# Half of the first feed-forward's gate product, by seven products of block sums instead of eight

## The chip, the cores and the metric

The kernel runs on one core of one Trainium2 chip. The metric is the device time in microseconds (us); three runs of the kernel before took 1800.26, 1800.73 and 1801.78 us, median 1800.73.

The engines are named as the profile names them: PE is TensorE (matrix multiplication), PEld its weight loading, DVE is VectorE, ACT is ScalarE, POOL is GpSimd, SP is SyncE, which here issues the DMAs (transfers from device memory). Each engine works through its own queue in order, and engines wait for each other on semaphores.

## The reference

Two blocks run one after the other on 512 tokens of 1024 features, in float32. Each feed-forward is two products with a gate between them; the change concerns the first one:

```python
def swiglu(x, w_gate, w_up, w_down):
    return (jax.nn.silu(x @ w_gate) * (x @ w_up)) @ w_down

def first_block(x, ...):
    ...                                   # input product, convolution and pooling groups
    h = h + y @ w_out[l]
    h = h + swiglu(rmsnorm(h, g_ffn[l]), w_gate[l], w_up[l], w_down[l])
    return rmsnorm(h, g_final)
```

`w_gate` and `w_up` are 1024 x 2816, `w_down` is 2816 x 1024. The second block has two layers of attention and feed-forward of the same sizes; they aren't touched.

## The kernel before

Features lie on the 128 partitions and tokens along the free dimension: `XH` and `XL` hold the normed input as eight tiles (the 1024 features) of 512 tokens. Precision comes from splitting each number in a high part, rounded to the matrix engine's format, and a low part, the remainder. A product is three matmuls: high weights by low input, high by high, low weights by high input (lines L983 to L985, helper `product`).

The stage "gu0" makes 22 tiles of gate and 22 of up, 128 hidden features each. One weight tile of 1024 x 128 is an *item*: 8 slices of the contraction by 3 matmuls, 24 matmuls of 512 tokens. Items come in the order gate, up, gate, up. The first two are made in halves of 256 tokens while the norm still delivers its halves (`stage_in_halves`, L1056 to L1069).

Each item passes through four engines:

- SP loads it to `raw`, which has 2 slots. Item g may be loaded when the low part of item g-2 is done (`w_lo`, helper `load`, L525 and L526).
- ACT rounds it to `WH` (helper `high`, two halves, L1605). It waits until it has landed and until PE is done with item g-4, as `WH` and `WL` have 4 slots.
- POOL subtracts to get `WL` (helper `low`, two halves, L742).
- PE multiplies.

Behind PE, ACT takes the silu of the gate bank (L1830), DVE multiplies it with the up bank to `hid` (L2428), ACT rounds that to `HH` (L1821) and POOL subtracts to `HL` (L869). `HH` and `HL` are the 22 hidden tiles that the product after this stage reads.

The norm ahead of the stage (`norm_in_halves`): DVE scales a tile of 256 tokens (L2156) into a small ring, ACT rounds to `XH` (L1658), POOL subtracts to `XL` (L783, `lows_of_halves`), and DVE may not go on with the ring until POOL has read it.

The order on each engine is written out by hand; in this stage it is a loop over pairs of tiles on every engine. Nothing reorders it.

Of the kernel before, what the change touches and what calls it, by code (L numbers as in the profile page):

```python
# [68 lines left out]

STAGES = {}  # L70
_item, _turn = 0, DT
for _name, _n, _t in (("in", 12, 12), ("out", 8, 8), ("gu0", 2 * FT, 2 * FT), ("down0", 8 * len(DOWN), 8),
                      ("qkv1", 4 * UNITS, 4 * UNITS), ("out1", 8, 8), ("gu1", 2 * FT, 2 * FT),
                      ("down1", 8 * len(DOWN), 8), ("qkv2", 4 * UNITS, 4 * UNITS), ("out2", 8, 8),
                      ("gu2", 2 * FT, 2 * FT), ("down2", 8 * len(DOWN), 8)):
    STAGES[_name] = (_item, _turn)
    _item, _turn = _item + _n, _turn + _t
# [88 lines left out]
class Chain:  # L166
# [9 lines left out]
    def sync(self, but=0):  # L176

        if self.it is None:
            self.eng.wait_ge(self.sem, self.count - but)
        else:  # L180
            self.eng.wait_ge(self.sem, self.it * self.per + self.count)
# [16 lines left out]
def two_blocks(nc, A, out):  # L198
    ctx = ExitStack()
    with ctx:  # L200
# [36 lines left out]
        pairs_of = [work[:, i, :].rearrange("p (a s) -> p a s", a=2) for i in (0, 1, 4)]  # L237
# [34 lines left out]
        ffn.close()  # L272
        att = ExitStack()
# [45 lines left out]
        sc = [pb("score0"), pb("score1")]  # L319
        tb = [pb("turned0"), pb("turned1")]  # L320
# [91 lines left out]
        slots = [*h_lo, *hid_ready, *ex, *pt_l, *o_read, qk_lo, sub_lo, sum_tiles]  # L412
# [60 lines left out]
        def ff_banks(it, j):  # L473

            return ob if isinstance(it, int) and j == 1 else bank

# [44 lines left out]
        def _(sp):  # L521
# [71 lines left out]
            stage("gu0", FT // 2, 4, pairs(w_gate, w_up))  # L593
# [135 lines left out]
        def _(pool):  # L729
# [143 lines left out]

            lows("out")
            lows_of_halves(1, "gu0")
            lows_of_hidden("gu0", 0)
# [104 lines left out]
        def _(pe):  # L981
# [97 lines left out]

            def gate_and_up(name, m):  # L1080

                stage_in_halves(name, m)
# [508 lines left out]
        def _(act):  # L1591
# [25 lines left out]
            def norm_in_halves(m, follower=None, gain=None):  # L1617
# [31 lines left out]
                def tops(h, p, tiles=range(2)):  # L1649
# [3 lines left out]
                    for t, w in TILES_OF_HALF:  # L1653
# [3 lines left out]
                        src = pairs_of[(DT * h + t) // 2 % 3][:, t % 2:t % 2 + w, :] if m == 1 else xres[:, t:t + w, c]  # L1657
# [160 lines left out]
            def hidden_hi(it, j, name):  # L1818

                act.wait_ge(bank_read[1], Nth(STAGES[name][1] + 2 * j + 1, it, 4).round(2, 1))  # L1820
                act.activation(HH[:, bass.ds(it * 2 + j, 1), :], hid[:, j:j + 1, :], ACT.Copy).then_inc(h_hi, 1)  # L1821
# [3 lines left out]
            def gate_hidden(it, j):  # L1825
                g = Nth(STAGES["gu0"][0] + 2 * j, it, 4)
                act.wait_ge(item_done, g.n(1))

                act.wait_ge(bank_read[1], Nth(STAGES["gu0"][1] + 2 * j + 1, it, 4).round(2, -1))
                act.activation(act_g[:, j, :], ff_banks(it, j)[0][:, :], ACT.Silu).then_inc(bank_read[0], 1)  # L1830
                high(g + 3)
                hidden_hi(it, j, "gu0")
                high(g + 4)

            for j in range(2):
                gate_hidden(0, j)
            with act.Fori(1, FT // 2) as it:
                for j in range(2):
                    gate_hidden(it, j)
# [232 lines left out]
        def _(dve):  # L2072
# [53 lines left out]
            def norm_in_halves(name, factor, gain, in_place=False):  # L2126
# [17 lines left out]
                def pair(h, p):  # L2144
                    c = slice(h * HALF, (h + 1) * HALF)
                    i = DT // 2 * h + p
                    dst = pairs_of[i % 3]
                    if p == 0:
                        dve.wait_ge(rstd_wide, stat(n, h))
                    if not centred:  # L2150
                        if i >= 3 and not in_place:
                            dve.wait_ge(x_lo, DT + half_tile(m, 0, 2 * (i - 3)) + 2)
                        for j in range(2):
                            t = 2 * p + j
                            x = xres[:, t, c]
                            dve.scalar_tensor_tensor(out=x if in_place else dst[:, j, :], in0=x, scalar=pcol(gain, t),  # L2156
# [266 lines left out]
            def gate_hidden(it, j):  # L2423
                g, u = Nth(STAGES["gu0"][0] + 2 * j + 1, it, 4), Nth(STAGES["gu0"][1] + 2 * j, it, 4)
# [257 lines left out]
```

## Time and profile before

| | |
|---|---|
| median of 3 runs | 1800.73 us |
| the profiled execution | 1802.1 us |
| its span | 1800.3 us |
| mean granted clock of TensorE | 0.995 |
| PE busy | 1761.6 us, 98% of the span |
| POOL, ACT, DVE busy | 1030.7, 796.4, 754.2 us (57%, 44%, 42%) |
| DMA | 171.93 MB, mean 96 GB/s |
| stage gu0 in this execution | 155.7 to 398.5 us |

Times in the profile are counted from the start of the span; 1.8 us of the execution lie outside it. A matmul's shown duration is longer than its distance from the next one, since matmuls are pipelined. So what a matmul costs is read from the distance between starts. The same holds in a smaller way for ACT and DVE: in a row "x2" the total is less than twice the duration of one.

### The profile page before, as it was taken

How to read it: one execution, taken by the hardware profiler on the slowest of the kernel's cores; microseconds unless marked ns; L12 is line 12 of the kernel's file. 1: busy time of each engine (PE TensorE's matmuls, PEld its weight loads, DVE VectorE, ACT ScalarE, POOL GpSimd, SP SyncE). 2: the span in 40 equal slices, each digit the busy share in tenths (PEclk: the TensorE clock that was granted, in tenths of full speed). 3: DMA queues.
4: the chain of work that ended last, by engine and by line, in shares of the span. 5: the costliest groups of instructions: out<-in, count | busy, mean ns of one | idle time of the engine just before them, and what ended most of it. 6: DMA issues, size and time to landing. Idle time of an engine off the chain costs nothing.

```text
span 1800.3 us, 26803 instructions
## 1 busy us (share of the span) xinstructions
PE 1761.6 (98%) x8755; PEld 1475.7 (82%) x8755; DVE 754.2 (42%) x1318; ACT 796.4 (44%) x1674; POOL 1030.7 (57%) x926
## 2 busy tenths in 40 slices
PE   8999999999999999999999999999999999999997
PEld 6879888888887888788888888878887888888887
DVE  7963000002235556453333322477875533333224
ACT  5644233232245555464444422466665644444231
POOL 6966555555562333466666665566564666666651
PEclk9999999999999999999999999999999999999999
DMA  4312333323234554323333333333332233332332
GB/s 153 94 44 80 104 101 93 93 79 114 87 88 114 136 123 122 88 72 109 100 93 95 88 105 92 87 82 88 88 84 79 71 106 93 96 102 79 105 92 98
DMA packets 327251, 171.93 MB, mean 96 GB/s; under 512 B 43458, under 2 KB 316948, under 8 KB 327188
## 3 DMA queue, kind: packets, MB, share of 16 engines
q1 hardware_dynamic: 327172, 171.12, 33.9%
q8 instruction: 35, 0.57, 0.1%
q14 instruction: 28, 0.23, 0.0%
q10 hardware_dynamic: 16, 0.00, 0.0%
HBM read 152.15 MB, written 2.10 MB: 86 GB/s over the span
## 4 chain that ended last, share of the span: by engine, by line
PE 86%; DVE 5%; POOL 3%; ACT 3%; issue 1%; DMA 1%; SPq 1%; DVEq 0%; ACTq 0%; POOLq 0%
PE bank L983 24%; PE bank L985 23%; PE bank L984 23%; PE attended L983 2%; PE attended L984 2%; PE attended L985 2%; PE turned L1424 1%; POOL WL L742 1%; PE attended L1440 1%; PE bank L1056 1%; PE bank L1068 1%; POOL psums L805 1%; ACT pmap L1861 1%; DVE small L2454 1%; DVE xres L2165 1%
## 5 line engine op out<-in xcount | busy, mean ns | idle before, releaser
L742 POOL TENSOR_TENSOR WL<-raw,WH 128x512 fp32r<-128x512 f32 (+3 forms) x656 | 775.7, 1204 | 540.9 <-ACT WH L1605 538.2
L983 PE MATMUL bank<-XL,WH 128*128 128x512 f32 x1432 | 568.4, 397 | 3.8 <-DVE work L2577 1.3
L985 PE MATMUL bank<-XH,WL 128*128 128x512 f32 x1432 | 557.6, 389 | 0.0
L984 PE MATMUL bank<-XH,WH 128*128 128x512 f32 x1432 | 556.9, 389 | 0.0
L1605 ACT ACTIVATE WH<-raw 128x512 fp32r<-128x512 f32 (+3 forms) x656 | 338.5, 566 | 296.3 <-PE bank L985 189.6
L985 PEld LDWEIGHTS bank<-XH,WL 128*128 128x128 f32 x1432 | 269.2, 188 | 56.9
L983 PEld LDWEIGHTS bank<-XL,WH 128*128 128x128 f32 x1432 | 269.7, 188 | 55.7 <-DVE work L2577 1.6
L984 PEld LDWEIGHTS bank<-XH,WH 128*128 128x128 f32 x1432 | 269.9, 188 | 50.2
L983 PE MATMUL bank<-HL,WH 128*128 128x512 f32 (+1 forms) x528 | 198.6, 376 | 0.0
L985 PE MATMUL bank<-HH,WL 128*128 128x512 f32 (+1 forms) x528 | 198.4, 376 | 0.0
L984 PE MATMUL bank<-HH,WH 128*128 128x512 f32 (+1 forms) x528 | 198.4, 376 | 0.0
L869 POOL TENSOR_TENSOR HL<-hid,HH 128x512 f32 x66 | 85.1, 1290 | 70.7 <-ACT HH L1821 70.7
L2366 DVE SCALAR_TENSOR_TENSOR xres<-xres,bank 128x512 f32 (+1 forms) x27 | 18.6, 687 | 249.7 <-PE bank L985 247.0
L983 PEld LDWEIGHTS bank<-HL,WH 128*128 128x128 f32 x528 | 99.4, 188 | 18.1
L984 PEld LDWEIGHTS bank<-HH,WH 128*128 128x128 f32 x528 | 99.4, 188 | 18.0
L985 PEld LDWEIGHTS bank<-HH,WL 128*128 128x128 f32 x528 | 99.3, 188 | 18.0
L1861 ACT ACTIVATE pmap<-score,small 128x128 f32<-128x128 f32 (+3 forms) x128 | 67.2, 525 | 93.6 <-DVE small L2454 92.2
L2428 DVE TENSOR_TENSOR hid<-bank,act_g 128x512 f32<-128x512 f32 x21 | 14.5, 692 | 207.5 <-PE bank L985 203.9
L1959 ACT ACTIVATE hid<-bank,par 128x512 f32<-128x512 f32 x42 | 32.7, 778 | 143.6 <-PE bank L985 143.6
L2514 DVE SCALAR_TENSOR_TENSOR hid<-bank,par,hid 128x511 f32<-128x511 f32 x42 | 31.5, 749 | 150.8 <-ACT hid L1959 150.6
L2514 DVE SCALAR_TENSOR_TENSOR act_g<-bank,par,act_g 128x511 f32<-128x511 f32 x42 | 31.5, 750 | 133.9 <-ACT act_g L1959 133.9
L2454 DVE TENSOR_REDUCE small<-score 128x1 f32<-128x128 f32 (+3 forms) x128 | 62.2, 487 | 40.1 <-PE score L1409 27.7
(365 smaller groups left out, 2508.7 us busy)
## 6 DMA issues: line engine op xcount, KB each, us to landing
raw<-in_ffn_w_in SPq DMA_DIRECT2D x88, 512.0 KB, 3.7
raw<-in_w_gate SPq DMA_DIRECT2D x22, 512.0 KB, 3.7
raw<-in_w_up SPq DMA_DIRECT2D x22, 512.0 KB, 3.7
raw<-in_ffn_w_out SPq DMA_DIRECT2D x28, 384.0 KB, 3.2
raw<-in_ffn_w_out SPq DMA_DIRECT2D x28, 320.0 KB, 3.1
raw<-in_a_w_in SPq DMA_DIRECT2D x16, 512.0 KB, 3.9
raw<-in_kv_w SPq DMA_DIRECT2D x32, 256.0 KB, 3.0
raw<-in_w_in SPq DMA_DIRECT2D x12, 512.0 KB, 3.7
```

Of the source, the lines that this page charges most:

```text
L742: pool.tensor_tensor(wl, x, wh, ALU.subtract).then_inc(w_lo, 1)
L805: own.link(pool.tensor_tensor(dst[:, PAD:], src[:, PAD:], src[:, PAD - d:PAD + S - d], ALU.add))
L869: pool.tensor_tensor(HL[:, bass.ds(it * 2 + j, 1), :], hid[:, j:j + 1, :], HH[:, bass.ds(it * 2 + j, 1), :].bitcast(F32), ALU.subtract).th ...
L983: pe.matmul(out_, wh, xl, start=start, stop=False)
L984: pe.matmul(out_, wh, xh, start=False, stop=False)
L985: return pe.matmul(out_, wl, xh, start=False, stop=stop)
L1605: act.activation(wh, x, ACT.Copy).then_inc(w_hi, 1)
L1861: act.activation(pmap[:, n % 4, 0:k], sc[c][:, 0:k], ACT.Exp, bias=small[:, n % 4:n % 4 + 1], accum_out=small[:, 4 + n % 4:5 + n % 4]).the ...
L1959: act.activation(dst[:, j, :], ff_banks(it, j)[side][:, :], ACT.Identity, bias=ff_par(layer - 1, 3, n), scale=ff_par(layer - 1, 2, n)).the ...
L2366: dve.scalar_tensor_tensor(out=r, in0=r, scalar=factor, in1=src[j][:, :].rearrange("p (a s) -> p a s", a=1), op0=ALU.mult, op1=ALU.add).th ...
L2454: dve.tensor_reduce(small[:, n % 4:n % 4 + 1], sc[c][:, 0:(n // 2 + 1) * P], AX_X, ALU.max, negate=True).then_inc(mx[c], 1)
L2514: own.link(dve.scalar_tensor_tensor(out=dst[:, j, 1:], in0=src[:, 0:S - 1], scalar=ff_par(layer - 1, 1, n), in1=dst[:, j, 1:], op0=ALU.mul ...
```

## The change

The input tiles 0 to 7 and the tokens form blocks: for a pair of input tiles (2k, 2k+1) and the two halves of the tokens, four blocks B11, B12, B21, B22; for two neighbouring gate tiles and the same two input tiles, four blocks of weights. The product of two such 2 x 2 arrangements is normally eight block products. In the variant of Winograd it is seven, of sums of blocks. A *quad* below is this for one k: seven products, each 3 matmuls of 256 tokens; four quads (k = 0 to 3) make the gate for two tiles. Seven of the eleven pairs of gate tiles (hidden tiles 2 to 15) are made so. Pair 0 and pairs 8 to 10, and all up tiles, are made as before.

What is added:

- Once: four sums of input blocks of 128x1024 on DVE (`turn_x`), their high parts on ACT (`turned_x_high`), their low parts on DVE (`turned_x_low`), between the norm and the first quad. They are kept in `TH` and `TL`, which are the hidden tiles 14 to 21 of `HH` and `HL`. The normed input is now written to `x_full` (hidden tiles 6 to 13), not to the ring.
- For each quad: a load of 256 KB (two input tiles by 256 weight columns) in place of one of 512 KB for each gate tile, so four small loads for two large ones; three sums and three plain blocks of weights. DVE makes four sums of weights in PSUM in three instructions (`quad_sums`) and their low parts (`sums_low`, 128x512); ACT makes the high parts of three plain blocks (`quad_high`, 128x384) and of the sums (`sums_high`, 128x512); POOL makes the low parts of the three plain blocks (`quad_low`, 128x384).
- For each pair: ACT copies the product P1 from PSUM (128x256), DVE combines the seven results in five instructions (`quad_answer`), then ACT takes the two silu.

```diff
-            stage("gu0", FT // 2, 4, pairs(w_gate, w_up))
+            folded("gu0", w_gate, w_up)
...
+                        if k < 4:
+                            src = wa[:, 2 * k:2 * k + 2, bass.ds(n, 2 * P)]
+                            sp.wait_ge(w_lo, g.times(2).n(2 * (1 - RAW)))
...
-                        src = pairs_of[(DT * h + t) // 2 % 3][:, t % 2:t % 2 + n, :] if m == 1 else xres[:, t:t + n, c]
+                        src = full_x(m)[:, t:t + n, c]
...
+                def quad(it, a):
+                    for k in range(4):
...
+                        for to, b, x, first in ((p1, 0, b11, True), (p2, 2, b21, True), (p4, 1, t4, True), (p7, 3, t3, True),
+                                                (p6, 5, t2, False), (p3, 6, b22, False), (p5, 4, t1, False)):
+                            if b == 0:
+                                if k == 0:
+                                    pe.wait_ge(quad_read, quad_count(name, it, a, 2).n() + OPEN)
+                                pe.wait_ge(w_lo, g.times(2).n(2))
+                            if b == 1 and k == 0:
+                                pe.wait_ge(t_lo, 4 * FOLDED.index(name) + 4)
+                            if b == 3:
+                                pe.wait_ge(sum_lo, q.n(1))
+                            mm = product(to, WHQ[:, s, b, :], WLQ[:, s, b, :], *x, first and k == 0, k == 3 and b >= 3)
...
+                item(Nth(STAGES[name][0] + 3), 0, XH, XL, 0, DT, True, True)
+                pe.wait_ge(bank_read[0], STAGES[name][1] // 2 + 2)
+                quad_pairs(pe.Fori, quad_pair)
...
+            def gate_quads(it, a, last):
...
+                high(quad_item("gu0", it, a, 4))
+                high(quad_item("gu0", it, a, 5))
...
+                    quad_high(next_item(0))
+                    sums_high(next_item(0), next_quad(0))
+                    quad_high(next_item(1))
+                act.wait_ge(item_done, quad_item("gu0", it, a, 3).n(1))
+                act.activation(p1_copy, ob[0][:, 0:HALF], ACT.Copy).then_inc(p1_out, 1)
                 for j in range(2):
-                    gate_hidden(it, j)
+                    act.wait_ge(quad_out, quad_count("gu0", it, a, 2, j).n(1))
+                    act.activation(act_g[:, j, :], answer[j][:, :], ACT.Silu).then_inc(quad_read, 1)
...
+                    sums_high(next_item(1), next_quad(1))
+                    quad_high(next_item(2))
+                hidden_hi(quad_tile(it, a, 0), 0, quad_turn("gu0", it, a, 0))
+                if not last:
+                    sums_high(next_item(2), next_quad(2))
+                    quad_high(next_item(3))
+                    sums_high(next_item(3), next_quad(3))
+                hidden_hi(quad_tile(it, a, 1), 1, quad_turn("gu0", it, a, 1))
...
+            def quad_sums(g, q):
+
+                r, to = raw[:, g.slot(RAW), 0:4, :], sums_of(q)
...
+                own.link(dve.tensor_tensor(to[:, 0:2, :], r[:, 0:1, :].broadcast_to([P, 2, P]), r[:, 1:3, :], ALU.add))
+                own.link(dve.tensor_tensor(to[:, 2, :], to[:, 1, :], r[:, 1, :], ALU.add))
+                dve.tensor_tensor(to[:, 3, :], to[:, 2, :], r[:, 3, :], ALU.add).then_inc(sum_ready, 1)
...
+                next_quad(0, quad_sums)
+                quad_answer("gu0", it, a)
+                next_quad(0, sums_low)
+                next_quad(1, quad_sums)
+                next_quad(1, sums_low)
+                next_quad(2, quad_sums)
+                value(0)
+                next_quad(2, sums_low)
+                next_quad(3, quad_sums)
+                value(1)
+                next_quad(3, sums_low)
```

On POOL a turn of the loop is `low` of the two up items, `quad_low` of the next quads 0 to 2, `HL` of the first hidden tile, `quad_low` of the next quad 3, `HL` of the second (`quad_lows`, `hidden_low`).

On PE, from the end of the fourth item on. Before, the loop over items of 512 tokens begins there:

```order
L985 MATMUL attended1<-XH,WL 128x512
L1085 UNCONDITIONAL_BRANCH
L1085 ISA
L990 ISA [waits bank_read0]
L983 MATMUL bank0<-XL,WH 128x512 [waits w_lo]
L984 MATMUL bank0<-XH,WH 128x512
L985 MATMUL bank0<-XH,WL 128x512
```

Now the first quad stands there (the first two of its seven products and the start of the third):

```order
L1127 MATMUL bank0<-XH,WL 128x512
L548 UNCONDITIONAL_BRANCH [waits bank_read0]
L548 ISA
L1238 ISA [waits quad_read]
L1125 MATMUL attended0<-XL,WH 128x256 [waits w_lo]
L1126 MATMUL attended0<-XH,WH 128x256
L1127 MATMUL attended0<-XH,WL 128x256
L1125 MATMUL turned<-XL,WH 128x256
L1126 MATMUL turned<-XH,WH 128x256
L1127 MATMUL turned<-XH,WL 128x256
L1125 MATMUL turned<-HL,WH 128x256 [waits t_lo]
```

The matmuls have 256 columns where they had 512, and there is a wait for the silu of the gate tile before (`bank_read0`), for the results' readers (`quad_read`), for the sums of the input (`t_lo`) and, three products on, for the sums of the weights (`sum_lo`). `HH` and `HL` stand for `TH` and `TL` here.

On ACT, from the norm's end to the first gate tile's silu and on. Before:

```order
L1658 ACTIVATE XH<-work 128x2x256 [waits xn_ready] x2
L1609 ACT_TABLE_LOAD
L1609 ACTIVATE small<-small 128x1
L1830 ACTIVATE act_g<-bank0 128x512 [waits bank_read1,item_done]
L1605 ACTIVATE WH<-raw 128x512 [waits item_done,w_landed1]
L1605 ACTIVATE WH<-raw 128x512
L1821 ACTIVATE HH<-hid 128x512 [waits bank_read1]
L1605 ACTIVATE WH<-raw 128x512 [waits item_done,w_landed0]
L1605 ACTIVATE WH<-raw 128x512
L1830 ACTIVATE act_g<-attended0 128x512 [waits bank_read1,item_done]
```

Now (from the same place; the norm, the table, item 3's high part and the high part of the first input sum stand ahead of these rows):

```order
L2035 ACTIVATE act_g<-bank0 128x512 [waits item_done]
L2023 ACTIVATE HH<-score 128x1024 [waits t_full]
L2013 ACTIVATE WH<-raw 128x384 [waits item_done,w_landed0]
L2023 ACTIVATE HH<-turned 128x1024 [waits t_full]
L2023 ACTIVATE HH<-score 128x1024 [waits t_full]
L2028 ACTIVATE HH<-hid 128x512 [waits bank_read1]
L2018 ACTIVATE WH<-score 128x512 [waits sum_ready]
L2013 ACTIVATE WH<-raw 128x384 [waits item_done,w_landed1]
L2018 ACTIVATE WH<-score 128x512 [waits sum_ready]
L2035 ACTIVATE act_g<-attended0 128x512 [waits item_done]
```

Between the silu of the first gate tile and that of the second there now stand the high parts of three of the input sums and of the first two quads, and the second silu (of `attended0`) is what `bank_read0` above waits for.

## Rows read from the trace of the kernel before

**Rows 1.** The page: busy time of each engine (share of the span), instructions

```profile
PE 1761.6 (98%) x8755; PEld 1475.7 (82%) x8755; DVE 754.2 (42%) x1318; ACT 796.4 (44%) x1674; POOL 1030.7 (57%) x926
```

**Rows 2.** Waits, 190 to 390 us: who for whom, us in total, times, longest

```profile
DVE hid L2428 <- PE bank L985: 193.8, 19, 10.4
```

**Rows 3.** PE in order of time: start, us, line, idle before in brackets

```profile
167.96 0.50 PE L1056 MATMUL bank<-XL,WH 128*128 128x256 f32 x2 [0.21 <-POOL XL L783]
169.98 0.40 PE L983 MATMUL attended<-XL,WH 128*128 128x512 f32 x1
...
180.89 0.39 PE L983 MATMUL bank<-XL,WH 128*128 128x512 f32 x1
...
398.49 0.39 PE L983 MATMUL bank<-HL,WH 128*128 128x512 f32 x1
```

**Rows 4.** PE in order of time, a stretch of matmuls of 256 columns

```profile
517.74 0.28 PE L984 MATMUL attended<-HH,WH 128*128 128x256 f32 x1
...
520.13 0.28 PE L1068 MATMUL bank<-XH,WH 128*128 128x256 f32 x1
```

**Rows 5.** DVE in order of time, 161 to 182 us

```profile
161.93 2.44 DVE L2156 SCALAR_TENSOR_TENSOR work<-xres,par,turned 128x256 f32<-128x256 f32 x6 [1.45 <-PE turned L1168]
...
166.22 0.48 DVE L2080 MEMSET work<- 128x512 f32 x1
...
170.86 0.69 DVE L2428 TENSOR_TENSOR hid<-bank,act_g 128x512 f32<-128x512 f32 x1 [3.61 <-ACT act_g L1830]
```

**Rows 6.** ACT in order of time, the first silu of the stage

```profile
170.06 0.60 ACT L1830 ACTIVATE act_g<-bank 128x512 f32<-128x512 f32 x1 [1.66 <-PE bank L1056]
```

**Rows 7.** POOL in order of time, 163 to 176 us

```profile
163.83 5.32 POOL L783 TENSOR_TENSOR XL<-work,XH 128x256 fp32r<-128x256 f32 x6
171.26 2.55 POOL L742 TENSOR_TENSOR WL<-raw,WH 128x512 fp32r<-128x512 f32 x2 [2.11 <-ACT WH L1605]
```

**Rows 8.** DVE in order of time, 504 to 507 us, where POOL works too

```profile
504.86 1.67 DVE L2373 TENSOR_TENSOR work<-work 128x512 f32<-128x512 f32 x1
```

**Rows 9.** POOL in order of time, 500 to 511 us

```profile
500.78 2.54 POOL L742 TENSOR_TENSOR WL<-raw,WH 128x512 fp32r<-128x512 f32 x2 [2.46 <-ACT WH L1605]
504.18 6.08 POOL L742 TENSOR_TENSOR WL<-raw,WH 128x512 fp32r<-128x512 f32 x4 [0.86 <-ACT WH L1605]
```

**Rows 10.** DVE groups by form: busy us, mean ns of one, idle before

```profile
L2458 DVE TENSOR_TENSOR PTL<-turned,PTH 128x512 fp32r<-128x512 f32 x24 | 16.4, 685 | 4.2 <-ACT PTH L1866 4.2
L2458 DVE TENSOR_TENSOR PTL<-turned,PTH 128x256 fp32r<-128x256 f32 x24 | 10.1, 421 | 5.7 <-ACT PTH L1866 5.7
L2458 DVE TENSOR_TENSOR PTL<-turned,PTH 128x128 fp32r<-128x128 f32 x24 | 6.9, 287 | 5.4 <-ACT PTH L1866 5.4
```

**Rows 11.** ACT groups by form, the same columns

```profile
L1727 ACT ACTIVATE work<-xin 128x1024 f32<-128x1024 f32 x4 | 4.2, 1058 | 2.7 <-DMA xin<-in_x 2.5
L1605 ACT ACTIVATE WH<-raw 128x384 fp32r<-128x384 f32 x111 | 54.3, 520 | 192.7 <-PE bank L985 152.9 <-DMA raw<-in_ffn_w_out 24.3 <-DMA raw<-in_w_down 15.6
L1866 ACT ACTIVATE PTH<-turned 128x256 fp32r<-128x256 f32 x24 | 9.0, 376 | 1.9 <-PE turned L1424 1.9
```

**Rows 12.** POOL in order of time, 385 to 440 us

```profile
400.50 1.29 POOL L869 TENSOR_TENSOR HL<-hid,HH 128x512 f32 x1 [3.44 <-ACT HH L1821]
...
433.29 1.99 POOL L742 TENSOR_TENSOR WL<-raw,WH 128x384 fp32r<-128x384 f32 x2 [1.92 <-ACT WH L1605]
```

**Rows 13.** ACT in order of time, the HH that Rows 12's first row waits for

```profile
399.68 0.63 ACT L1821 ACTIVATE HH<-hid 128x512 f32 x1 [4.71 <-DVE hid L2428]
```

**Rows 14.** DMA issues: KB each, us from issue to landing

```profile
raw<-in_w_gate SPq DMA_DIRECT2D x22, 512.0 KB, 3.7
...
raw<-in_kv_w SPq DMA_DIRECT2D x32, 256.0 KB, 3.0
...
QX<-work SPq DMA_DIRECT2D x32, 128.0 KB, 2.3
...
raw<-in_b_w_q SPq DMA_DIRECT2D x16, 256.0 KB, 3.3
```

More of the change, by code:

```diff
@@ L180, in sync @@
         else:
-            self.eng.wait_ge(self.sem, self.it * self.per + self.count)
+            self.eng.wait_ge(self.sem, self.it * self.per + (self.count - but))
     def link(self, ins):
@@ L475, in ff_banks, with t_banks, quad_item, quad_turn @@
             return ob if isinstance(it, int) and j == 1 else bank
+        folds, p1_copy = [work[:, 0, :], work[:, 1, :]], work[:, 4, 0:HALF]
+        answer = [tb[1], folds[0]]
+        def t_banks(n):
+            x = turned2 if n in (2, 0) else score2
+            return x[:, :, :].rearrange("p b s -> p (b s)").rearrange("p (k c) -> p k c", c=HALF)
+        turn_of_sums = [x.rearrange("p (b c) -> p b c", c=P) for x in sc]
+        def quad_item(name, it, a, k):
+            return Nth(STAGES[name][0] + 4 + QUAD_ITEMS * a + k, it, 2 * QUAD_ITEMS)
+        def quad_turn(name, it, a, j):
+            return Nth(STAGES[name][1] + 4 + 2 * a + j, it, 4)
+        def quad_count(name, it, a, per, k=0):
+            return Nth(per * (QUADS * FOLDED.index(name) + a) + k, it, 2 * per)
+        def plain_item(name, it, k):
+            return Nth(STAGES[name][0] + (QUAD_ITEMS - 4) * QUADS + k, it, 4)
+        def plain_turn(name, it, k):
+            return Nth(STAGES[name][1] - 2 * QUADS + k, it, 4)
+        def quad_tile(it, a, j):
+            return bass.ds(it * 4 + (2 * a + 2 + j), 1)
+        def sums_of(q):
+            return turn_of_sums[q.slot(2)]
+        def full_x(m):
+            return x_full if m == 1 else xres
+        def quad_pairs(Fori, part):
+            with Fori(0, QUAD_LOOP) as it:
+                for a in range(2):
+                    part(it, a, False)
+            part(QUAD_LOOP, 0, True)
         def first_unit(u):
@@ L1835, in _, with quad_high, sums_high @@
-            for j in range(2):
-                gate_hidden(0, j)
-            with act.Fori(1, FT // 2) as it:
-                for j in range(2):
-                    gate_hidden(it, j)
+            def quad_high(g):
+                s = g.slot(SLOTS)
+                act.wait_ge(w_landed[g.slot(RAW)], g.round(RAW, 1) * 16)
+                act.wait_ge(item_done, g.n(1 - SLOTS))
+                act.activation(WHQ[:, s, 0:3, :], raw[:, g.slot(RAW), 1:4, :], ACT.Copy).then_inc(w_hi, 1)
+            def sums_high(g, q):
+                act.wait_ge(sum_ready, q.n(1))
+                act.activation(WHQ[:, g.slot(SLOTS), 3:7, :], sums_of(q), ACT.Copy).then_inc(w_hi, 1)
```

277 lines of the change are left out of this document (242 added, 35 removed).

## The prediction

> **What bounds the kernel now.** I read the page first: PE is busy for 98% of the span, POOL for 57%, no other engine for half [rows 1]. Then the waits inside the stage: DVE waits for PE for 193.8 us in 200, and no row there has PE waiting for anyone [rows 2]. So at present every matmul taken out of this stage shortens the kernel by its full distance to the next, and the other engines have air. Then PE in order of time, to get prices and the stage's edges. The halves end at 169.98 (PE waited 0.21 us for POOL's `XL` shortly before), the fourth item ends at 180.89, the stage at 398.49 [rows 3]. Between 180.89 and 398.49 stand 40 items of 24 matmuls: 217.60 / 960 = 0.2267 us each, 5.44 us an item, 21.76 us a pair of tiles.
>
> **The price of a matmul of 256 columns.** From 517.74 to 520.13 there are 20 of them, 0.1195 us each [rows 4]. That is 5% more than half of 0.2267, so halving the columns costs something.
>
> **What is taken from PE.** For a pair the gate was 48 x 0.2267 = 10.88 us. Now it is 4 quads x 21 matmuls x 0.1195 = 10.04 us. The gain is 0.84 us for a pair, 5.9 us for seven. This is all that can be won: 0.33% of the kernel. What can be told from no change here is about 0.2%, 3.6 us. So 2.3 us of new waits on PE already hide the gain.
>
> **The start of the first quad.** Three things are new there.
>
> - DVE scales eight tiles for the second half of the tokens from 161.93 on, 2.44 / 6 = 0.41 us each, without the ring's wait now: until 165.2, with two fills of 0.48 us until 166.2 [rows 5]. Then comes the first sum of inputs, 128x1024 with both inputs in SBUF, while POOL makes the `XL` that PE waits for (its row runs from 163.83 to 169.15) [rows 7]. A DVE instruction of that kind took 1.67 us beside a busy POOL, where the same size with one input in PSUM takes 0.69 [rows 8, 10]; POOL needed 6.08 us for the four subtractions around it and 2.54 for two undisturbed ones, so it lost 1.0 [rows 9]. I read it as a lock: each waits for the other's instruction to end. The new sum is about 1.2 us long (0.685 at 512, and 0.26 more for each 256 [rows 10]), and POOL, and with it PE, come 1.2 us later: the halves end at 171.2, item 3 at 182.1.
> - The Trainium skill, SBUF — State Buffer, section "SBUF: two separate sides", states this as a rule: the port pair is an exclusive lock for a whole instruction, also for a DVE instruction with two SBUF inputs against a GpSimd one that reads SBUF. By that rule, the trace agrees; without it the end of the sum below would be 2.7 us earlier.
> - The chain to the first quad. DVE's first `hid` began 0.88 us after the halves' end [rows 3, 5], now at 172.1, and takes 0.69. Behind it stand two more input sums and four low parts, six instructions of 1024 at 1.24: 180.2. ACT's four high parts (1.06 each [rows 11]) fit between. Then the sums of quads 0 and 1, each 0.42 + 0.29 + 0.29 and small gaps, 1.05: 182.3. ACT makes the high part of quad 1's sums (0.60, as a read of PSUM [rows 6]) and only then the silu of `attended0` (0.60), for which PE waits: with three handovers 183.8. PE stands still for 1.7 us. The quads start 2.9 us later than their place before.
>
> If nothing else waited, the stage would end at 183.8 + 7 x (10.04 + 10.88) + 12 x 5.44 = 395.5, which is 3.0 us sooner.
>
> **The ring behind PE.** A pair now asks PE for 20.92 us only. But the preparation of one pair hangs in a ring, because each engine works in order: two `raw` slots, ACT's silu between weight copies, DVE's sums between answers. I walk it once, from POOL's first half of the first up item's low part to the same one of the next pair:
>
> 1. POOL, four half subtractions of 1.27 [rows 9]: 5.1 us. They free the slot for quad 1's load.
> 2. The load of 256 KB. Not in this form in the trace: 512 KB take 3.7, 256 KB in short rows 3.0 to 3.3, 128 KB in long rows 2.3 [rows 14]. The new one has rows of 1 KB, twice as long as the loads of 3.0; I take 2.5, nearer the long rows, and 2.7 with the handovers.
> 3. ACT: quad 1's plain high part, 0.42 to the next start (0.52 long), and the P1 copy, 0.38, queued behind it [rows 11]; with the handover 0.95. The copy was possible at the end of quad 3, and waits here for a load it has no need of.
> 4. DVE's five instructions of the answer: 0.69, 0.42, 0.42, 0.69, 0.42, with the overlap of independent ones 2.5 [rows 10].
> 5. DVE: low part of quad 0's sums 0.62, sums of quad 1 1.05: 1.7.
> 6. ACT's high part of these sums 0.60, two handovers, DVE's low part 0.62: 1.4.
> 7. DVE: sums of quad 2 1.05, `hid` 0.69: 1.7.
> 8. ACT: `HH` 0.53, high part of quad 2's sums 0.60, handovers: 1.35.
> 9. DVE: low part 0.62, sums of quad 3 with a wait of 0.25 for POOL 1.3, `hid` 0.69: 2.6.
> 10. ACT's `HH` 0.63, POOL's `HL` 1.29, handovers of 0.14, an estimate, and 0.19 (400.31 to 400.50) [rows 12, 13]: 2.25. Then POOL is at step 1 again.
>
> The sum is 22.25. The second up item's high part comes 0.15 late for POOL (its load starts only after POOL's last part of quad 3): 22.4 us a turn. That is 1.5 more than PE asks for, and 0.6 more than the 21.76 of before. For the first turn there is slack; then PE waits each turn, at quad 3 (POOL's part), at the first up item and at the next first quad.
>
> **The sum.** In pair 0, quad 2's load goes out when POOL is done with quad 0 (182.6) and lands at 185.2; its sums and low part take until 187.4 (1.05, then 1.0, half of the 1.99 for two of 128x384 [rows 12]); the up item's load (3.7) lands at 191.2; POOL starts on it at 192.0. Six turns later, at 192.0 + 134.4 = 326.4, POOL starts on the last quad pair's up item, PE on it 1.3 us later, and from there nothing waits: 14 items x 5.44 = 76.2. The stage ends at 403.9, against 398.5: 5.4 us later. Behind it PE still has no slack, so all of it reaches the end. The profiled execution (span 1800.3 and 1.8 around it, 1802.1) would come to 1807.5; it lies 1.4 us above the median, so the median is forecast at 1806.1 us.
>
> **Bounds.** The load between 2.3 (128 KB in long rows) and 3.3: minus 0.2 to plus 0.8 a turn. The Trainium skill, DMA: Bandwidth & Descriptors, section "Anatomy of one DMA", fits about 2.0 us plus the bytes at 436 GB/s, which would be 2.6 here and 0.6 us more in the sum; its 3.2 for 512 KB is under the measured 3.7. The ten handovers I set at 0.06 to 0.15, under the two that rows show (0.20 from 170.66 to 170.86 [rows 5, 6], and the 0.19 above); 0.05 more or less for each is 0.5 a turn either way. No wait for POOL at step 9: minus 0.25. So a turn is 21.45 to 23.7, and six turns move the end from 5.7 us below the forecast to 7.8 above it. At the low bound the ring gives 398.2, no change.
>
> **Rivals.**
>
> - *PE stays the limit* (the ring at 20.9 or less): 395.5, minus 3.0, 1797.7 us; if the start cost nothing as well, minus 5.9, 1794.8. For it: ACT's, DVE's and POOL's work for a pair sums to about 10, 12 and 12 us, none near 21. Against it: it isn't the sums that bind but the order in which they wait for each other.
> - *The ring is about as long as a pair was* (21.5 to 22.0): 1800 to 1804, no change to be told. For it: both handovers that the rows show stand where an engine has several waits or an address to work out, and a plain one may be shorter than I set it. This is the nearest case.
> - *The matmuls of 256 columns cost more in the loop than at 517 us*, since each quad has its own waits: 588 of them at 0.130 would be 6.2 us more and eat the whole gain with PE itself as the limit, 1804. Against it: the cost of a satisfied wait can't be seen in 40 items at 5.44. That the seven products bring less than 1/8 is the same question; the difference in count is certain.
> - *A longer load decides* (3.0 or more, as 256 KB in short rows): a turn of 22.9, plus 8.4, 1809.
>
> **How the numbers follow.** The forecast case with the longer load (slower by over 0.2%): 0.55. Of that the longer load is 0.15. No change, mostly the second rival: 0.31. PE the limit and the start cheaper than worked out, by which alone more than 3.6 us are won: 0.14. The range reaches from 1798.5 to 1811.5: below it lies most of "PE stays the limit", above it only both upper bounds at once. The likeliest case's own range is 1804.3 to 1811.
>
> **What would show it.** In the profile after: 588 matmuls of 256 columns in the stage at about 0.12 apart (else the gain is wrong). PE idle about 1.2 us more for `XL` near 168, and about 1.7 us for the silu of `attended0` near 182. From the second quad pair on, PE idle in each turn behind POOL's low parts, and a pair every 22.4 us; if a pair takes 20.9, the ring is wrong and the kernel is not slower. The load of 256 KB at 2.5. DVE's 1024-wide sum at 167 longer than 1.2. All stages behind as long as before; if they aren't, I have missed something outside the stage.

## The result, and the profile after

| | median, us | runs | ratio to before |
|---|---|---|---|
| before | 1801.26 | 4 | |
| changed | 1812.38 | 4 (1809.86 to 1812.68) | 1.0058 (1.0040 to 1.0075) |
| changed, once more, later | 1811.08 | 4 (1806.45 to 1811.84) | 1.0048 (1.0031 to 1.0065) |

The ratios are taken over all runs of both kernels and can differ a little from the quotient of the two medians. The kernel became slower by about 0.5%. 1806.1 was forecast, with 1811.5 as the upper end: the sign was right, the size about half of what was measured.

The profiled execution of after took 1809.86 us, with a span of 1808.0. Its first 160 us (the front), where the work on TensorE is the same, ran 2.1 us faster than in the profile of before, so times are compared from a point of the stage on. Most of that is TensorE's clock: the granted clock was 0.50, the level of 1.2 GHz, from 103.7 to 110.5 us in before's execution and from 104.8 to 108.2 in after's, with TensorE busy throughout, and half of the 3.4 us between the two is 1.7 us of its work. In the stage itself neither profile has such a stretch. The page of after, which answers to [rows 1]:

```profile
PE 1757.2 (97%) x9007; PEld 1479.2 (82%) x9007; DVE 831.0 (46%) x1473; ACT 818.5 (45%) x1713; POOL 1026.0 (57%) x927
```

PE is busy for 4 us less, in a span that is 8 us longer. The waits of after, 160 to 420 us (who for whom, us in total, times, longest), answer to [rows 2]:

```profile
PE attended L1125 <- POOL WL L978: 4.4, 6, 0.8
PE attended L1125 <- ACT act_g L2058: 2.8, 5, 1.1
PE bank L1125 <- DVE hid L2737: 1.7, 1, 1.7
PE bank L1125 <- POOL WL L841: 1.5, 6, 0.4
```

Before, PE waited in this stretch for `XL` only, 0.4 us in all. Now PE waits in every turn of the ring for POOL (L978, L841), in five of them for the silu (L2058), and once at its end (`hid`). The 1.3 us for `XL` and the 1.2 for the second silu of the start (L2035) come on top. PE in order of time, as in [rows 3] (start, duration, and the idle time before in brackets):

```profile
166.79 0.51 PE L1198 MATMUL bank<-XL,WH 128*128 128x256 f32 x2 [1.17 <-POOL XL L882]
168.81 0.40 PE L1125 MATMUL attended<-XL,WH 128*128 128x512 f32 x1
...
181.04 0.38 PE L1125 MATMUL attended<-XL,WH 128*128 128x256 f32 x1 [1.16 <-ACT act_g L2035]
...
247.96 0.38 PE L1125 MATMUL attended<-XL,WH 128*128 128x256 f32 x1 [0.39 <-ACT act_g L2058]
256.16 0.39 PE L1125 MATMUL attended<-XL,WH 128*128 128x256 f32 x1 [0.78 <-POOL WL L978]
259.08 0.50 PE L1125 MATMUL bank<-XL,WH 128*128 128x512 f32 x1 [0.18 <-POOL WL L841]
...
340.22 0.49 PE L1125 MATMUL bank<-XL,WH 128*128 128x512 f32 x1 [1.69 <-DVE hid L2737]
...
405.63 0.39 PE L1125 MATMUL bank<-HL,WH 128*128 128x512 f32 x1
```

I call the time from the product that waits for `XL` (here 166.79) to the first product with `HL` (405.63) the stage's length. It was 398.49 - 167.96 = 230.53 us before and is 238.84 now, 8.3 more; with 1.0 more of wait ahead of it the change costs 9.3 us. Behind the stage 1402.4 us remain, against 1401.8 before.

The ring, read from POOL's first part of the first up item of each pair (first, second and last of the seven):

```profile
189.50 5.05 POOL L841 TENSOR_TENSOR WL<-raw,WH 128x512 fp32r<-128x512 f32 x4 [0.54 <-ACT WH L1795]
211.61 2.53 POOL L841 TENSOR_TENSOR WL<-raw,WH 128x512 fp32r<-128x512 f32 x2
...
325.94 2.54 POOL L841 TENSOR_TENSOR WL<-raw,WH 128x512 fp32r<-128x512 f32 x2
```

Six turns take 136.44 us, 22.74 each. The loads, 180 to 330 us (KB each, us from issue to landing), answer to [rows 14]:

```profile
raw<-in_w_up SPq DMA_DIRECT2D x14, 512.0 KB, 3.6
raw<-in_w_gate SPq DMA_DIRECT2D x26, 256.0 KB, 2.7
```

One turn on ACT (from the plain high part of the next quad 0 to the silu of this pair) and on DVE:

```profile
240.42 0.53 ACT L2013 ACTIVATE WH<-raw 128x384 fp32r<-128x384 f32 x1 [2.00 <-DMA raw<-in_w_gate]
241.58 0.60 ACT L2018 ACTIVATE WH<-score 128x512 fp32r<-128x512 f32 x1 [0.63 <-DVE score L2704]
243.55 0.53 ACT L2013 ACTIVATE WH<-raw 128x384 fp32r<-128x384 f32 x1 [1.38 <-DMA raw<-in_w_gate]
243.99 0.36 ACT L2055 ACTIVATE work<-attended 128x256 f32<-128x256 f32 x1
246.72 0.60 ACT L2058 ACTIVATE act_g<-turned 128x512 f32<-128x512 f32 x1 [2.36 <-DVE turned L2728]
```

```profile
244.48 0.69 DVE L2724 TENSOR_TENSOR work<-work,turned 128x512 f32<-128x512 f32 x1 [2.94 <-ACT work L2055]
```

The third and fourth rows of ACT are the heart of it. The P1 copy (L2055) comes right behind a weight part that waited 1.38 us for its load, and DVE stood still for 2.94 us until the copy was there.

### The profile page after: what moved, and what is told of

Read it like the earlier page. It is cut to its first block, busy times and chain, and to the rows that moved or that the text cites. A ratio compares the mean times of both kernels' runs of the same rounds, so it can differ in the third digit from the quotient of the medians.

```text
span 1808.0 us, 27685 instructions
## 1 busy us (share of the span) xinstructions
PE 1757.2 (97%) x9007; PEld 1479.2 (82%) x9007; DVE 831.0 (46%) x1473; ACT 818.5 (45%) x1713; POOL 1026.0 (57%) x927
## 4 chain that ended last, share of the span: by engine, by line
PE 78%; DVE 8%; POOL 5%; ACT 3%; issue 3%; DMA 2%; DVEq 0%; SPq 0%; POOLq 0%; ACTq 0%
PE bank L1125 21%; PE bank L1127 21%; PE bank L1126 21%; POOL WL L841 3%; PE attended L1125 2%; PE attended L1127 2%; PE attended L1126 2%; PE turned L1614 2%; PE attended L1630 1%; DMA raw<-in_w_gate 1%; PE bank L1198 1%; PE bank L1210 1%; POOL psums L904 1%; DVE score L2702 1%; DVE xres L2418 1%
## 5 line engine op out<-in xcount | busy, mean ns | idle before, releaser
L841 POOL TENSOR_TENSOR WL<-raw,WH 128x512 fp32r<-128x512 f32 (+2 forms) x628 | 741.5, 1203 | 529.3 <-ACT WH L1795 527.0
L1125 PE MATMUL bank<-XL,WH 128*128 128x512 f32 (+1 forms) x1328 | 528.6, 398 | 7.3 <-POOL WL L841 2.0
L1127 PE MATMUL bank<-XH,WL 128*128 128x512 f32 (+1 forms) x1328 | 517.1, 389 | 0.0
L1126 PE MATMUL bank<-XH,WH 128*128 128x512 f32 (+1 forms) x1328 | 516.5, 389 | 0.0
L1795 ACT ACTIVATE WH<-raw 128x512 fp32r<-128x512 f32 (+2 forms) x628 | 322.5, 563 | 317.4 <-PE bank L1127 178.8
L1125 PEld LDWEIGHTS bank<-XL,WH 128*128 128x128 f32 x1328 | 250.1, 188 | 56.9 <-POOL WL L841 3.1
L1127 PEld LDWEIGHTS bank<-XH,WL 128*128 128x128 f32 x1328 | 249.7, 188 | 53.1
L1126 PEld LDWEIGHTS bank<-XH,WH 128*128 128x128 f32 x1328 | 250.3, 188 | 45.7
L978 POOL TENSOR_TENSOR WL<-raw,WH 128x384 fp32r<-128x384 f32 x28 | 28.5, 1016 | 71.2 <-DVE score L2704 71.2
L882 POOL TENSOR_TENSOR XL<-xres,XH 128x256 fp32r<-128x256 f32 (+1 forms) x48 | 43.7, 923 | 38.0 <-ACT XH L1848 38.0
```

The costliest lines, as they stand in the source:

```text
L841: pool.tensor_tensor(wl, x, wh, ALU.subtract).then_inc(w_lo, 1)
L882: pool.tensor_tensor(XL[:, t:t + n, c], src, XH[:, t:t + n, c].bitcast(F32), ALU.subtract).then_inc(x_lo, n)
L978: pool.tensor_tensor(WLQ[:, s, 0:3, :], raw[:, g.slot(RAW), 1:4, :], WHQ[:, s, 0:3, :].bitcast(F32), ALU.subtract).then_inc(w_lo, 2)
L1125: pe.matmul(out_, wh, xl, start=start, stop=False)
L1126: pe.matmul(out_, wh, xh, start=False, stop=False)
L1127: return pe.matmul(out_, wl, xh, start=False, stop=stop)
```

## The experiments

"Stage" is the length defined above. "PE waits" is the sum of the rows of PE in the waits, 150 to 420 us, the one for `XL` included. "Turn" is the mean of the six turns in the profile. The kernels ran in groups beside runs of before, whose medians are 1801.93 (23 runs, for e1 to e4), 1802.84 (21, e5 to e8) and 1802.07 (7, e9 and e10).

| kernel | median | ratio (interval) | stage | PE waits | turn |
|---|---|---|---|---|---|
| changed | 1812.38 | 1.0058 (1.0040 to 1.0075) | 238.84 | 12.9 | 22.74 |
| e1_copy_ahead | 1799.75 | 0.9985 (0.9975 to 0.9994) | 229.97 | 5.6 | 21.19 |
| e2_last_ahead | 1808.38 | 1.0028 (1.0015 to 1.0041) | 237.28 | 11.2 | 22.80 |
| e3_three_pairs | 1807.01 | 1.0028 (1.0018 to 1.0037) | 235.19 | 6.2 | |
| e4_silu_ahead | 1813.05 | 1.0062 (1.0045 to 1.0079) | 242.85 | 14.8 | 23.07 |
| e5_both_orders | 1797.09 | 0.9974 (0.9963 to 0.9984) | 226.32 | 2.6 | 20.99 |
| e6_all_waits | 1797.90 | 0.9977 (0.9965 to 0.9988) | 228.66 | 3.1 | 20.93 |
| e7_sum_behind_xl | 1812.55 | 1.0050 (1.0034 to 1.0067) | 240.94 | 12.7 | 22.71 |
| e8_half_load | 1806.41 | 1.0014 (1.0004 to 1.0023) | 234.56 | 9.5 | 22.13 |
| e9_start_in_order | 1794.54 | 0.9958 (0.9941 to 0.9975) | 224.98 | 1.5 | 20.96 |
| e10_changed_again | 1811.08 | 1.0048 (1.0031 to 1.0065) | 238.27 | 11.8 | 22.61 |

### The copy ahead of the load (e1)

```diff
+                def copy_p1():
+                    act.wait_ge(item_done, quad_item("gu0", it, a, 3).n(1))
+                    act.activation(p1_copy, ob[0][:, 0:HALF], ACT.Copy).then_inc(p1_out, 1)
...
                     quad_high(next_item(0))
                     sums_high(next_item(0), next_quad(0))
+                    copy_p1()
                     quad_high(next_item(1))
-                act.wait_ge(item_done, quad_item("gu0", it, a, 3).n(1))
-                act.activation(p1_copy, ob[0][:, 0:HALF], ACT.Copy).then_inc(p1_out, 1)
```

(In the last pass `copy_p1` stays where it was.)

> ACT's copy of P1 stands ahead of the plain high part of the next pair's quad 1, so it no longer waits for that quad's load; the last pair is as it was. Theory (the ring through POOL, DMA, ACT and DVE sets the stage's pace, and this copy is a link of it): a turn of the ring, read as the distance of POOL's first subtraction of a pair's first up item to the next pair's, falls by about 1.5 us from 22.7 to 21.2; PE's waits at a next first quad and at quad 3 shrink, and the stage is about 7 us shorter than in the changed kernel, which leaves it 2 to 4 us slower than before. Rival 1 (the matmuls of 256 columns or the start cost it): nothing moves in the loop, under 0.5 us. Rival 2 (the slot of the raw weights alone sets the pace): the turn stays at 22.7, because the loads go out when they did.

The turn is 21.19 us, as the theory had it, and of the ring's waits of PE 1.3 us of 8.7 are left in the whole stage. The stage is 8.9 us shorter, where 7 were expected, so the kernel isn't 2 to 4 us slower than before but a little faster. The same place on ACT:

```profile
301.35 0.53 ACT L2013 ACTIVATE WH<-raw 128x384 fp32r<-128x384 f32 x1 [1.94 <-DMA raw<-in_w_gate]
302.50 0.60 ACT L2018 ACTIVATE WH<-score 128x512 fp32r<-128x512 f32 x1 [0.62 <-DVE score L2708]
302.99 0.38 ACT L2049 ACTIVATE work<-attended 128x256 f32<-128x256 f32 x1
304.30 0.53 ACT L2013 ACTIVATE WH<-raw 128x384 fp32r<-128x384 f32 x1 [0.92 <-DMA raw<-in_w_gate]
305.83 0.60 ACT L2062 ACTIVATE act_g<-turned 128x512 f32<-128x512 f32 x1 [1.00 <-DVE turned L2732]
```

The copy no longer has a load in front of it, the answer is made while that load is under way, and the silu comes 4.5 us behind the first row where it came 6.3 behind. No instruction is saved and none made shorter. One instruction in another place moved the kernel from 0.5% slower to 0.15% faster, so the order, and not the work, set the length of a turn.

### The last pair (e2)

```diff
                 if last:
-                    high(next_item(0))
-                    high(next_item(1))
-                else:
+                if not last:
...
                 if last:
+                    high(next_item(0))
+                    high(next_item(1))
                     high(next_item(2))
```

> In the last pair of quads only, ACT's two rounds of the next plain items' weights are put behind the copy of P1 and the two silu. Theory (the 1.7 us that PE waited for DVE's hid at 340 us came from the copy queued behind two weight loads that had not landed): that wait goes, the stage is 1.7 to 2.1 us shorter than in the changed kernel and nothing else moves, ring turns stay at 22.7. Rival (PE waited there for weights as well, which now come later): the wait is replaced by one for POOL's subtraction of the first plain item, gain under 0.5 us.

The wait for `hid` at the end of the ring is gone from PE's waits, and the turns are as long as in the changed kernel. The stage is 1.6 us shorter (1.0 against e10's). The two medians differ by more, 2.7 to 4.0 us, which the profiles don't account for; the execution profiled here was the slowest of e2's eight (1811.46). What happened there, in the last pass of the changed kernel (ACT, then DVE):

```profile
332.36 1.16 ACT L1795 ACTIVATE WH<-raw 128x512 fp32r<-128x512 f32 x2 [3.28 <-DMA raw<-in_w_gate]
335.01 1.15 ACT L1795 ACTIVATE WH<-raw 128x512 fp32r<-128x512 f32 x2 [1.50 <-DMA raw<-in_w_up]
336.07 0.37 ACT L2055 ACTIVATE work<-attended 128x256 f32<-128x256 f32 x1
338.71 0.60 ACT L2058 ACTIVATE act_g<-turned 128x512 f32<-128x512 f32 x1 [2.27 <-DVE turned L2728]
```

```profile
336.47 0.69 DVE L2724 TENSOR_TENSOR work<-work,turned 128x512 f32<-128x512 f32 x1 [12.03 <-ACT work L2055]
...
339.40 1.29 DVE L2737 TENSOR_TENSOR hid<-bank,act_g 128x512 f32<-128x512 f32 x2 [0.40 <-issue]
```

The copy stands behind the weights of two plain items, each with a load of 512 KB. `hid` begins at 339.40, and PE's next item needs the bank that `hid` reads. It is the ring's fault once more, with larger loads.

### Three pairs in place of seven (e3)

```diff
-QUADS = 7
+QUADS = 3
```

> Three pairs of gate tiles in place of seven are made by seven products; five more than before by eight. Theory (a pair by quads takes 22.7 us on the ring against 21.76 by plain items, plus a fixed cost of start and end of about 4 us): the stage ends about 4 us sooner than with seven pairs, and about 5 us later than before (+0.3%). Rival (the loss lies at the start and the end only and each pair of quads still saves its 0.84 us): the stage ends 3.4 us later than with seven pairs, about 12.5 us later than before.

The total came near what was expected, 3.65 us less in the stage than with seven pairs, but not by the parts. Its two turns took 21.25 and 21.74 us (the changed kernel's first two: 22.11 and 23.40), and PE's wait for `hid` behind the last pair was 3.1 us instead of 1.7. So the loss is not in proportion to the pairs: start and end cost as much with three of them. Behind that wait the granted clock was 0.50 from 248.2 to 251.6 us, which is another 1.7 us of PE's work and not the change's. Beyond that this run settles little.

### The second silu first (e4)

```diff
+            first_gate(1)
             sums_high(quad_item("gu0", 0, 0, 0), quad_count("gu0", 0, 0, 4, 0))
             quad_high(quad_item("gu0", 0, 0, 1))
             sums_high(quad_item("gu0", 0, 0, 1), quad_count("gu0", 0, 0, 4, 1))
-            first_gate(1)
```

> ACT takes the silu of the second gate tile (bank attended0) before the high parts of the first quads' sums, so PE's wait of 1.2 us ahead of the first quad should go. Theory (from the second pair on the ring sets the pace, and the ring's start hangs on the sums and loads, not on PE): PE's wait goes, the first quads run 1.2 us sooner, and the slack is used up at the second pair: the stage ends within 0.4 us of the changed kernel. Rival (PE's own waits add up, whatever stands behind): the stage is 1.2 us shorter.

The wait of 1.16 us went, and nothing was won: PE came earlier to the first up item, and waited for it.

```profile
191.14 0.50 PE L1125 MATMUL bank<-XL,WH 128*128 128x512 f32 x1 [0.97 <-POOL WL L841]
```

The stage in this profile is 4.0 us longer than the changed kernel's, where at most 0.4 was expected, though the median lies only 0.7 higher. Two parts can be read. The first two turns were 0.9 and 1.3 us longer. And from 343.3 to 346.7 us, right behind PE's wait of 1.8 us for `hid`, the granted clock was 0.50: from POOL's start on the last pair's up item to the end of the stage it took 81.4 us instead of 79.7. So this run shows that the silu's wait is replaced by another; to 0.4 us, what the move gives can't be read from it.

### The load's length (e8)

```diff
-                            src = wa[:, 2 * k:2 * k + 2, bass.ds(n, 2 * P)]
+                            src = wa[:, 2 * k:2 * k + 1, bass.ds(n, 2 * P)]
...
-                            sp.dma_start(raw[:, g.slot(RAW), 0:4, :].rearrange("p (k n) c -> p k (n c)", k=2),
+                            sp.dma_start(raw[:, g.slot(RAW), 0:2, :].rearrange("p (k n) c -> p k (n c)", k=1),
```

> The changed kernel, but each load of a gate tile of a pair brings the first two of its four blocks only, 128 KB in place of 256 KB; what is computed from the others is not the reference's. All instructions of the engines stay. The theory (one load stands in each turn of the ring): a load of about 2.3 us instead of 2.7, so turns of about 22.3 instead of 22.74 and six of them 2.5 us shorter: 1809.9 us, ratio 1.004 to 1.0055. The rival (the turn is bound by the work of ScalarE, VectorE and GpSimd in their order, with the load beside it): turns of 22.7 us and 1812.4.

```profile
raw<-in_w_gate SPq DMA_DIRECT2D x26, 128.0 KB, 2.0
```

The load is 0.7 us shorter (0.4 was expected), a turn 0.61 (0.48 against e10), and that with every instruction of every engine as it was and the loads of `w_up` at 3.6 us as before. The second turn, 23.4 us, didn't gain; the last four are 21.95 us against 22.73 (22.58 in e10), so 0.6 to 0.8 each. So the theory holds over the rival: about one such load stands in each turn. The median fell by 6.0 us (4.7 against e10), where six turns give 3.7; the rest isn't explained.

### Both orders (e5)

The edits of e1 and e2 together.

> The changed kernel with both orders of ScalarE: in the ring the copy of P1 stands ahead of the weights of the next pair's second tile, and in the last pass the weights of the three plain tiles stand behind the two silus. The theory (ring, and a last pass with the same fault): turns of 21.0 to 21.2 us as with the copy ahead alone, and of TensorE's idle time in the stage the 1.9 us before the first plain tile goes as well, so about 1.8 us below the copy alone (1799.75): 1798 us, ratio 0.997 to 0.999. The rival (the two are one loss, and the end is bound by the weights of the plain tiles): no change to the copy alone, 1799.8, and a wait for the split of w_up or w_gate stands where the wait for hid was.

The turn is 20.99 us, where the arithmetic of PE alone gives 20.92. The wait for `hid` is gone, and in the whole stage PE waits for these only:

```profile
PE bank L1198 <- POOL XL L882: 1.2, 1, 1.2
PE attended L1125 <- ACT act_g L2035: 1.2, 1, 1.2
PE bank L1125 <- POOL WL L841: 0.2, 1, 0.2
```

The stage is 3.7 us shorter than in e1: 1.9 is the wait, 1.2 a turn that in e1's profile took 22.0. The median lies 2.7 us lower, with intervals that overlap.

### The wait for XL (e7, e6)

```diff
+            dve.wait_ge(x_lo, DT + half_tile(1, 1, DT - 1) + 1)
             turn_x(2, full_x(1), 1)
...
-            turned_x_high("gu0", 2)
             first_gate(0)
+            turned_x_high("gu0", 2)
```

e6 has this on top of e5, and `first_gate(1)` ahead of the second quad's weights.

> The changed kernel with one edit: VectorE's first sum of inputs waits until GpSimd is through with XL, and the first silu stands ahead of the copy of that sum. Theory (the two engines hinder each other where VectorE reads two tensors from SBUF): six low parts in 5.3 us instead of 6.30, VectorE's sum in 1.22 instead of 1.47, TensorE's wait for XL 0.2 instead of 1.17. Rival (the low parts are slower for another cause, such as ScalarE's writes beside them): 6.3 and 1.17 stay. In the time the ring theory expects under 1 us of it, since the ring behind the start goes on at its own pace: 1811 to 1812.5 us, ratio 1.005 to 1.006.

> As both orders, and two waits of the start taken away: VectorE makes the first sum of inputs only when GpSimd is through with the low parts XL (and ScalarE does the first silu ahead of the copy of that sum), and the second silu of the start stands ahead of the second pair of weight tiles instead of behind. The theory: the wait for XL falls from 1.17 to about 0.2 us, the six low parts from 6.30 to 5.3 us, and the wait for the second silu from 1.16 to 0.3 or less; together about 1.9 us below both orders: 1796 us, ratio 0.996 to 0.998. The rival (what the start wins is taken up by the first loads of the ring, as where the silu alone went ahead and nothing was won): the time of both orders within 0.5 us.

First the changed kernel (POOL, then DVE), then e7 (the same):

```profile
161.68 6.30 POOL L882 TENSOR_TENSOR XL<-x_full,XH 128x256 fp32r<-128x256 f32 x6
...
164.14 1.47 DVE L2682 TENSOR_TENSOR turned<-x_full 128x1024 f32<-128x1024 f32 x1
```

```profile
163.57 5.34 POOL L882 TENSOR_TENSOR XL<-x_full,XH 128x256 fp32r<-128x256 f32 x6
...
169.05 2.21 DVE L2682 TENSOR_TENSOR turned<-x_full 128x1024 f32<-128x1024 f32 x1 [3.05 <-POOL XL L882]
```

In the changed kernel POOL's row of six took 6.30 us. In e7 it takes 5.34, and PE's longest wait for `XL` is 0.2 instead of 1.17: that the two engines hinder each other is shown, and the price is 0.96 on POOL, where 1.2 had been worked out. But nothing was won. Stage and the wait ahead of it together are 1.1 us longer than in the changed kernel (e7), and 1.4 longer than in e5 (e6). The first input sum now comes 3 us later and falls on POOL's next weight part, so DVE needs 2.21 us where 1.22 was expected, and the chain of sums behind it slips as a whole. In e7 PE waited 3.7 us for the second silu, and in e6 2.7 us for the first quad's weights. So e6's theory, 1.9 us below both orders, failed: at 1797.9 it lies 0.8 above them, near what the rival said (the same within 0.5), though not by the rival's mechanism. In both profiles the granted clock also fell to 0.50 behind PE's wait, from 181.8 to 185.2 us in e6 and from 185.6 to 189.0 in e7. That is 1.7 us of PE's work and no part of the edit. The delay of the sums shows without it: counted from the end of the front, the first quad's sums came 1.6 us later in both, and POOL's start on the first up item 1.6 and 1.7.

### The start in another order (e9), the fastest

```diff
             turned_x_high("gu0", 2)
-            first_gate(0)
             turned_x_high("gu0", 3)
+            first_gate(0)
...
-            first_hidden(0)
             turned_x_low("gu0", 2)
+            first_hidden(0)
```

And `first_gate(1)` as in e4, on top of e5.

> Both orders of ScalarE in the ring and in the last pass, and the start written in another order, with no wait added: VectorE takes the low parts of the first sum of inputs before the first hidden tile instead of behind it, ScalarE copies the second sum before the first silu, and the second silu stands ahead of the first sums of weights. The theory (VectorE idles 2.69 us before the first hidden tile, and the chain of sums behind it sets when the first pair's weights and the loads behind them come): the chain starts 1.2 us earlier, the first weight part of an up tile of the first pair too (POOL at 188.2 against 189.43), the wait of 1.16 for the second silu is gone, and with the ring free of waits all of it reaches the end: 1.2 us below both orders, 1795.9 us, ratio 0.996 to 0.9975. The rival (the start is set by the loads, and what it wins comes back as a wait at the first up tile): POOL at 189.4 as before, a wait of about 1 us at the first up tile, and 1797 us.

```profile
PE bank L1198 <- POOL XL L882: 1.3, 2, 1.2
PE bank L1125 <- POOL WL L841: 0.2, 1, 0.2
```

The second silu's wait is gone, and no other of more than 0.2 us took its place; POOL reaches the first up item 21.5 us behind the product that waited for `XL`, instead of 22.7. The start's three edits came together here, so the silu's share isn't shown by itself; together they shorten the stage by 1.3 us against e5 (1.2 was expected). In e4 the same move of the silu, with the ring behind it, brought nothing. The stage is 224.98 us long, 5.5 shorter than before; 5.9 were there to be won. With 1.0 more of wait for `XL` ahead, 4.5 us are accounted for. The median says 7.5 (interval 4.5 to 10.6), so up to 3 us of it I can't place; the profiled execution's first 160 us were 3.2 us faster than in the profile of before, and it has no stretch at a granted clock of 0.50 near 104 us.

### The changed kernel again (e10)

No edit.

> The changed kernel as it is, once more beside the others of this call. All theories: the ring of 22.7 to 22.8 us a turn, a wait of 1.7 us for hid after the last pair, 1811 to 1812.6 us, ratio 1.0045 to 1.006.

All as in the first runs. One execution of its four took 1806.45, the one profiled; its turns were 22.61. A single time of this kernel can be over 4 us off the median.

## Why the prediction was wrong in size

Point by point, with after's times moved by the 2.1 us of its faster front:

- *The price of 256 columns* held. In e5, where nothing else waits, a turn is 20.99 against 20.92 worked out. The rival of dear small matmuls is out.
- *The lock* held: 1.0 more on PE for 1.2 worked out, DVE's sum 1.47 for 1.22, and e7 takes it away by making DVE's sum wait. Step 9's 0.25 for POOL is there too: the first sums of quad 3 took 0.65 us (at 321.76), and 0.42 undisturbed.
- *The second silu* held: 1.16 of idle, for 1.7 worked out.
- *The first up item* on POOL at 191.6 for 192.0: minus 0.4.
- *The ring* held as a mechanism: e1 takes it away by moving one copy, e8 shortens it by its load. Its size was set too low, 22.4 for 22.74, so plus 2.0 in six turns. The load was taken at 2.5 and took 2.7: 1.2 in six turns. POOL's wait for the second up item's weights, set at 0.15 a turn, was 0.86, 0.43, 0.33, 0.40 and 0.63 us in turns two to six and nothing in the first: 1.8 more. The other steps must then have been about 1 us shorter in all than set; I haven't told them apart. The estimate of 2.6 from the Trainium skill's fit (DMA: Bandwidth & Descriptors, section "Anatomy of one DMA") was nearer than my choice; for 512 KB the fit gives 3.2 against a measured 3.6. But that section is about transfers issued by GpSimd, and these are issued by SyncE, which the prediction did not say.
- *"From there nothing waits"*, in the sum, is the step that failed. From POOL's start on the last pair's up item, PE was taken to run free for 1.3 + 76.2 us; it took 79.7 (325.94 to 405.63): 2.2 more. 1.7 of it is the wait at 340.22, and e2 takes that wait away; 0.1 lies at its start (327.37), and 0.4 stands in no wait that the rows show. I had followed the copy behind a load through every turn of the ring, and did not read the branch `if last`, where the same copy stands behind two larger loads.
- *The base* was a second mistake: the median was taken 1.4 us under the profiled execution of before, from three runs. Later groups of 7 to 23 runs have it at 1801.9 to 1802.8, which is where that execution lay. This deduction had nothing behind it.

So the stage cost 9.3 us where 5.4 were forecast (-0.4, +2.0, +2.2, and 0.1 of rounding), and 1.4 came off that should have stayed: 1802.1 + 9.3 = 1811.4, where 1812.38 and 1811.08 were measured. Of the range, the upper end was said to need "both upper bounds at once". It needed neither. The measured 1812.38 lies 6.3 above the forecast: 2.2 by a wait that the sum put at nothing, 2.0 by the turns, 1.4 by the base, less 0.4 at the start, 0.1 of rounding, and 1.0 that I can't place. Without any one of the first three it would have been inside the range, and two of them, the wait and the base, had been given no bound.

## What to carry to other kernels

In an engine that works in order, ask of every short instruction that another engine waits for what stands ahead of it in its queue, and whether that waits for a load; if so, the load's time is in the loop. Do the same walk for the first and the last pass, whose code is another branch: what binds the loop binds there too, with other sizes. Taking a wait away brings its time only where nothing behind it is paced by something else: the silu's place brought nothing in e4, with the ring behind it, and the start's new order brought 1.3 us in e9, without the ring.

## What was not expected of the hardware

- DVE and POOL hinder each other for about a whole instruction. In e6 POOL began two subtractions at 166.08 and DVE its sum at 166.26. POOL's two took 3.53 us, against 2.54 alone; DVE's sum took 2.21, against 1.22. Each paid 0.99 more. If DVE had waited for POOL's first to end (166.08 + 1.27 = 167.35), and POOL's second for DVE's (167.35 + 1.22 = 168.57), DVE would have paid 1.09 and POOL 1.22, so a lock gives both to within 0.25 us. The Trainium skill states it as a lock (SBUF — State Buffer, section "SBUF: two separate sides").

```profile
166.08 3.53 POOL L841 TENSOR_TENSOR WL<-raw,WH 128x512 fp32r<-128x512 f32 x2
```

```profile
166.26 2.21 DVE L2686 TENSOR_TENSOR turned<-x_full 128x1024 f32<-128x1024 f32 x1 [3.04 <-POOL XL L882]
```

- The time from issue to landing of a load of weights was 2.0 us for 128 KB and 2.7 for 256 KB (both in rows of 1 KB), and 3.6 for 512 KB in rows of half that length. The 128 KB of [rows 14] took 2.3, so two transfers of one size can differ by 0.3.
- Executions of one kernel differ by up to 8 us (before, beside e1 to e4: 1799.45 to 1807.71), and go with the mean granted clock of TensorE: of before's runs beside e1 to e4 those at 0.997 took 1800.1 on average (3 runs), those at 0.995 1802.2 (10), the one at 0.992 1804.8, the one at 0.989 1807.7.
- In the profiles part of this scatter shows as single stretches at a granted clock of 0.50, the level of 1.2 GHz, which lie at other times in each execution. Before has one at 103.7 to 110.5 us, after one at 104.8 to 108.2, e9 and e10 none there; before and e9 also have one at 15 to 18 us, after and e10 don't. Without the last wait for `XL`, the front took 167.8, 165.6, 164.5 and 163.5 us in these four (before, after, e9, e10). Near 104 us TensorE had been busy for over 3 us when the clock fell. In e3, e4, e6 and e7 it fell inside the stage, within 1.2 us of the end of a wait of 3.1, 1.8, 2.7 and 3.7 us, for 3.4 us each time; behind the waits of 1.6 to 1.9 us in the changed kernel, e1, e8 and e10 it did not. What sets it off is not shown.
